# Rings of two to four buffers for the modulation pieces, and another spread of their sums over the stages

## The reference

```python
for layer in range(2):
    sh_m, sc_m, g_m, sh_f, sc_f, g_f = split(cond @ ada_w[layer] + ada_b[layer], 6)
    h = rms_norm(x, norm_w[layer, 0]) * (1.0 + sc_m) + sh_m
    y = even_mixer(h) if layer == 0 else odd_mixer(h)   # mLSTM + forgetting attention; GLA
    x = x + g_m * rms_norm(y, norm_w[layer, 1])
    h = rms_norm(x, norm_w[layer, 2]) * (1.0 + sc_f) + sh_f
    y = conv_ffn(h)          # 2048 -> 2 x 5632, causal conv of 3, a * gelu(g), 5632 -> 2048
    x = x + g_f * rms_norm(y, norm_w[layer, 3])
```

## Time and profile before

| | |
|---|---|
| Median of 3 runs | 2491.28 us (2486.13 to 2492.52) |
| Profiled execution, its own time | 2495.06 us |
| Its span | 2493.2 us |
| PE busy | 2389.3 us, 96% |
| DVE busy | 1994.6 us, 80% |
| ACT busy | 1007.4 us, 40% |
| DMA | 627 MB, 251 GB/s over the span |
| Granted clock of PE, mean | 0.990 |

### The profile page before, as it was taken

How to read it: one execution, slowest core, us unless ns; L and a number is a source line. 1 busy time by engine, 2 the same in 40 slices (tenths; PEclk the granted TensorE clock), 3 DMA queues, 4 the chain that set the end, 5 groups by cost and what they waited for, 6 DMA issues and landing times.

```text
span 2493.2 us, 36131 instructions
## 1 busy us (share of the span) xinstructions
PE 2389.3 (96%) x13994; PEld 2108.8 (85%) x13994; DVE 1994.6 (80%) x2531; ACT 1007.4 (40%) x1028; POOL 221.5 (9%) x111
## 2 busy tenths in 40 slices
PE   7999989799999999999989999998999999999998
PEld 6878877699988999799878888887888888888886
DVE  6779987789977998789777767777888778877875
ACT  2134444353333343333445544454444334433443
POOL 0000000024410443024200000000000000000000
PEclk9999999999999999999999999999999999999999
DMA  9999966857788777877858644466455865576553
GB/s 400 413 366 354 353 224 240 287 192 271 273 301 301 275 276 287 308 284 277 301 188 305 228 152 140 148 236 237 169 185 186 296 225 185 185 257 248 183 188 136
DMA packets 114466, 627.03 MB, mean 251 GB/s; under 512 B 12768, under 2 KB 12960, under 8 KB 63152
## 3 DMA queue, kind: packets, MB, share of 16 engines
q1 hardware_dynamic: 113648, 621.22, 68.5%
q10 hardware_dynamic: 704, 4.23, 0.4%
HBM read 623.27 MB, written 2.13 MB: 251 GB/s over the span
## 4 chain that ended last, share of the span: by engine, by line
PE 71%; DVE 15%; DMA 10%; ACT 3%; issue 1%; SPq 0%; DVEq 0%; ACTq 0%
PE bank L1760 17%; PE bank L1761 16%; PE bank L1756 7%; PE bank L1757 7%; PE bank L1784 7%; PE bank L1786 7%; PE bank L1785 7%; DMA piece<-ada_pieces 6%; DVE lo L934 5%; DVE piece L945 3%; DMA region<-ada_pieces 3%; ACT hi L507 2%; PE bank L1666 1%; DVE y L945 1%; PE bank L1540 1%
## 5 line engine op out<-in xcount | busy, mean ns | idle before, releaser
L507 ACT ACTIVATE hi<-raw 128x2048 fp32r<-128x2048 f32 x378 | 724.4, 1917 | 1116.4 <-PE bank L1761 678.8
L1761 PE MATMUL bank<-act,lo 128*128 128x256 f32 x3616 | 1020.1, 282 | 0.0
L934 DVE TENSOR_TENSOR lo<-raw,hi 128x2048 fp32r<-128x2048 f32 x378 | 864.9, 2288 | 144.2 <-ACT hi L507 143.3
L1761 PEld LDWEIGHTS bank<-act,lo 128*128 128x128 f32 x3616 | 690.0, 191 | 0.1
L1760 PE MATMUL bank<-act,hi 128*128 128x512 f32 x1920 | 678.0, 397 | 3.0 <-DVE lo L934 2.5
L1756 PE MATMUL bank<-act,hi 128*128 128x256 f32 x1696 | 485.0, 286 | 8.2 <-DVE lo L934 7.2
L1757 PE MATMUL bank<-act,hi 128*128 128x256 f32 x1696 | 481.7, 284 | 0.0
L945 DVE SCALAR_TENSOR_TENSOR piece<-piece,cond 128x1024 f32<-128x1024 f32 x290 | 398.0, 1375 | 83.2 <-DMA piece<-ada_pieces 83.0
L1760 PEld LDWEIGHTS bank<-act,hi 128*128 128x128 f32 x1920 | 360.3, 188 | 90.5 <-DVE lo L934 3.4
L1756 PEld LDWEIGHTS bank<-act,hi 128*128 128x128 f32 x1696 | 327.7, 193 | 11.5 <-issue 5.3
L1757 PEld LDWEIGHTS bank<-act,hi 128*128 128x128 f32 x1696 | 327.6, 193 | 0.1
(11 more groups left out here) (184 smaller groups left out, 1966.7 us busy)
## 6 DMA issues: line engine op xcount, KB each, us to landing
raw<-w_units SPq DMA_DIRECT2D x378, 1024.0 KB, 4.9
piece<-ada_pieces SPq DMA_DIRECT2D x290, 512.0 KB, 5.2
region<-ada_pieces SPq DMA_DIRECT2D x64, 512.0 KB, 13.9
raw<-head_units SPq DMA_DIRECT2D x16, 1024.0 KB, 16.0
y<-ada_pieces SPq DMA_DIRECT2D x30, 512.0 KB, 6.4
region<-gamma_scratch ACTq DMA_DIRECT2D x4, 1024.0 KB, 6.7
x<-x_in SPq DMA_DIRECT2D x1, 2048.0 KB, 9.2
x_out<-x SPq DMA_DIRECT2D x3, 512.0 KB, 2.8
```

The costliest lines, as they stand in the source:

```text
L507: sc.activation(hi[:, slot, :], raw[:, raw_slot, :], ACT.Copy).then_inc(s_hi, 1)
L934: ve.tensor_tensor(lo[:, slot, :], raw[:, raw_slot, :], hi[:, slot, :].bitcast(F32), ALU.subtract).then_inc(s_lo, 1)
L1761: i_ = pe.matmul(dst, w_lo, act[:, kt, 0:T], start=False, stop=at == DK - 1)
```

## The change

The pieces get ten slots in place of four, and each phase names a ring of them. Slots 0 and 1 are `piece`; 2, 3 and 7 lie in `y`; 4 and 5 in the place of the gamma row; 6 is `extra`; 8 and 9 are the places of the first GLA heads' queries and keys. The first `mixed` and the last first-layer `ff_down` have rings of three, the other two first-layer `ff_down` and the second `mixed` rings of four, the first `ff_up` and the decay phase of three, the GLA phases rings of two, other two than before. A slot is opened once by a load at a given place behind a wait for its last user, and after that each load follows the sum of the piece that lay in the slot before, even over phases.

The places of the sums move too. First-layer `ff_up` groups sum 24, 16 and 12 pieces where it was 32, 32 and 24. The first two `ff_down` sum 30 each where it was 24. The GLA phases sum 16 and 8 where it was none. All other counts stay. With three pieces per body the first `ff_up` is written out in full and not looped.

```diff
-    no, down = (0,) * 4, (1, 2, 2, 1) * 4
+    no, down = (0,) * 4, (1, 2, 2, 2, 2, 2, 2, 2) * 2
...
-              Phase("mixed", 0, 1, 16, (0, 0, 0, 1, 1, 2, 2, 2, 2, 2, 2, 2, 2, 2, 0, 0)),
-              Phase("ff_up", 0, 8, 4, (1,) * 4, 0), Phase("ff_down", 0, 1, 16, down, 0),
-              Phase("ff_up", 0, 8, 4, (1,) * 4, 1), Phase("ff_down", 0, 1, 16, down, 1),
-              Phase("ff_up", 0, 6, 4, (1,) * 4, 2),
-              Phase("ff_down", 0, 1, 12, (1, 2, 2, 1, 2, 2, 1, 2, 2, 1, 0, 0), 2),
+              Phase("mixed", 0, 1, 16, (0, 0, 0, 1, 1, 2, 2, 2, 2, 2, 2, 2, 2, 2, 0, 0), ring=(0, 1, ROWS)),
+              Phase("ff_up", 0, 8, 4, (1, 1, 1, 0), 0, ring=(0, 1, GAMMA)),
+              Phase("ff_down", 0, 1, 16, down, 0, ring=(0, 1, GAMMA, GAMMA + 1)),
+              Phase("ff_up", 0, 8, 4, (1, 0, 1, 0), 1),
+              Phase("ff_down", 0, 1, 16, down, 1, ring=(0, 1, GAMMA, GAMMA + 1)),
+              Phase("ff_up", 0, 6, 4, (1, 0, 1, 0), 2),
+              Phase("ff_down", 0, 1, 12, (1, 2, 2, 1, 2, 2, 1, 2, 2, 1, 0, 0), 2, ring=(0, 1, ROWS)),
...
-              Phase("columns", 1, 4, 4, (2, 1, 2, 1), dest=GQ, side="decay"),
-              Phase("values", 1, 2, 8, (0,) * 8, side="gla"),
-              Phase("columns", 1, 2, 8, (0,) * 8, dest=GR, side="gla", side0=2),
-              Phase("mixed", 1, 1, 16, (0, 0, 0, 0, 1, 1, 1, 2, 2, 2, 2, 2, 2, 1, 0, 0)),
+              Phase("columns", 1, 4, 4, (2, 1, 2, 1), dest=GQ, side="decay", ring=(0, 1, GAMMA)),
+              Phase("values", 1, 2, 8, (1,) * 8, side="gla", ring=STORED),
+              Phase("columns", 1, 2, 8, (0, 0, 1, 1, 1, 1, 0, 0), dest=GR, side="gla", side0=2, ring=HEADS),
+              Phase("mixed", 1, 1, 16, (0, 0, 0, 0, 1, 1, 1, 2, 2, 2, 2, 2, 2, 1, 0, 0), ring=HEADS + (0, 1)),
...
+        if ph.per_body % 2:
+            ph.head = ph.bodies
...
+OPENS = {(5, ROWS), (6, GAMMA), (7, GAMMA + 1), (11, ROWS), (13, GAMMA), (14, 3), (14, 7), (15, 8), (15, 9),
+         (16, 0), (16, 1)} | {(1, k) for k in EARLY}
+
+def piece_plan():
+    slots, uses, follows, opened = {}, {}, {}, {}
+    last, count = {}, [0] * ADA_SLOTS
+    for n, ph in enumerate(PHASES):
+        for a in range(ph.a0, ph.a_end):
+            slot = ph.ring[(a - ph.a0) % len(ph.ring)]
+            if (n, slot) in OPENS and last.get(slot, 0) < ph.a0:
+                opened[n, slot] = a
+            else:
+                follows[last[slot]] = a
+            slots[a], uses[a], last[slot] = slot, count[slot], a
+            count[slot] += 1
+    return slots, uses, follows, opened
...
-        pieces = [piece[:, 0, :], piece[:, 1, :], yf[:, 0:PIECE], yf[:, PIECE:2 * PIECE]]
+        pieces = [piece[:, 0, :], piece[:, 1, :], yf[:, 0:PIECE], yf[:, PIECE:2 * PIECE],
+                  gamma_row[:, 0:PIECE], gamma_row[:, PIECE:2 * PIECE], extra[:, :], yf[:, 2 * PIECE:3 * PIECE],
+                  region[:, GQ * T:GQ * T + PIECE], region[:, GK * T:GK * T + PIECE]]
...
+            def open_slots(number, ph, j):
+                if number == 5 and j == 0:
+                    sp.wait_ge(s["mlstm_scores_ready"], M_HEADS)
+                    load_piece(OPENED[5, ROWS], ROWS)
+                if number == 6 and j == 0:
+                    sp.wait_ge(s_yg, CHUNKS + 1)
+                    load_piece(OPENED[6, GAMMA], GAMMA)
+                if number == 7 and j == 0:
+                    load_piece(OPENED[7, GAMMA + 1], GAMMA + 1)
+                if number == 11 and j == 0:
+                    sp.wait_ge(s_evac, 2 + ph.t0)
+                    load_piece(OPENED[11, ROWS], ROWS)
+                if number == 13 and j == 0:
+                    sp.wait_ge(s_yg, 2 * (CHUNKS + 1))
+                    load_piece(OPENED[13, GAMMA], GAMMA)
+                    sp.wait_ge(s_act, 2 * 8)
+                    for slot in STORED:
+                        load_piece(OPENED[14, slot], slot)
+                if number == 15 and j == 1:
+                    sp.wait_ge(s["gla_level_product"], 2 * (LEVELS + 1))
+                    for slot in HEADS:
+                        load_piece(OPENED[15, slot], slot)
+                if number == 16 and j == 2:
+                    sp.wait_ge(s["gla_attended"], G_HEADS)
+                    for slot in PAIR:
+                        load_piece(OPENED[16, slot], slot)
...
                         for _ in range(ph.ada[j]):
                             a = ph.a0 + i * ph.per_body + k
...
+                            if ahead[k] > 0:
                                 sp.wait_ge(s_mac, a + 1)
-                                load_piece(a + ahead, slot)
+                                load_piece(a + ahead[k], ph.ring[k % len(ph.ring)])
                             k += 1
```

More of the change, by code:

```diff
@@ L45 @@
 SECTIONS = 6 * LAYERS
-ADA_SLOTS, EARLY_SLOTS = 2, 4
 HEAD_SLOTS = 8
@@ L55, with __init__ @@
 class Phase:
-    def __init__(self, kind, layer, bodies, units, ada, group=0, dest=0, side=None, side0=0):
+    def __init__(self, kind, layer, bodies, units, ada, group=0, dest=0, side=None, side0=0, ring=(0, 1)):
         self.kind, self.layer, self.bodies, self.units, self.ada = kind, layer, bodies, units, ada
@@ L147, with last_use, piece_ahead, even_loads @@
 PAUSE = next(ph for ph in PHASES if ph.side == "gla").a0
-EARLY_END = next(ph for ph in PHASES if ph.side == "mlstm").a0
-assert (EARLY_END - 2 * PIECES) % EARLY_SLOTS == 0
-def piece_slot(ph, k):
-    a = ph.a0 - 2 * PIECES + k
-    if ph.a0 < EARLY_END:
-        assert ph.bodies == 1 or ph.per_body % EARLY_SLOTS == 0
-        return a % EARLY_SLOTS, a // EARLY_SLOTS, ph.per_body // EARLY_SLOTS
-    early = EARLY_END - 2 * PIECES
-    return ((a - early) % ADA_SLOTS, early // EARLY_SLOTS + (a - early) // ADA_SLOTS, ph.per_body // ADA_SLOTS)
+FIRST = 2 * PIECES
+OPENS = {(5, ROWS), (6, GAMMA), (7, GAMMA + 1), (11, ROWS), (13, GAMMA), (14, 3), (14, 7), (15, 8), (15, 9),
[4 more added lines that the diff above has]
+    for n, ph in enumerate(PHASES):
+        assert ph.per_body % len(ph.ring) == 0 or ph.bodies == 1 or ph.side == "mlstm"
+        for a in range(ph.a0, ph.a_end):
[6 more added lines that the diff above has]
+            count[slot] += 1
+    assert set(opened) == OPENS
+    return slots, uses, follows, opened
+SLOT, USE, FOLLOWS, OPENED = piece_plan()
+def last_use(slot, before):
+    return max(a for a in SLOT if SLOT[a] == slot and a < before)
+def piece_ahead(ph, i):
+    return [FOLLOWS.get(a, a) - a for a in range(ph.a0 + i * ph.per_body, ph.a0 + (i + 1) * ph.per_body)]
+def even_loads(ph):
+    return all(piece_ahead(ph, i) == piece_ahead(ph, ph.head) for i in range(ph.head, ph.bodies - ph.peel))
 V_ADAB = 0
@@ L454, in _, with body @@
             sp.wait_ge(s_hact, DK)
[L455 to L456 removed]
+            for slot in EARLY[2:4]:
+                load_piece(FIRST + slot, slot)
             sp.wait_ge(s_lo, RAW_SLOTS + 1)
             load_unit(RAW_SLOTS, 0)
[L460 to L461 removed]
+            def open_slots(number, ph, j):
[24 more added lines that the diff above has]
+                        load_piece(OPENED[16, slot], slot)
+            for number, ph in enumerate(PHASES):
+                def body(i, ph=ph, number=number):
+                    ahead = piece_ahead(ph, ph.now)
                     k = 0
@@ L489, in _ @@
                     sp.wait_ge(s["mlstm_stored"], 2 + M_HEADS)
+                    sp.wait_ge(s_mac, last_use(ROWS, PAUSE) + 1)
                     sp.dma_start(g_w2, w2_dram).then_inc(s["loaded_a_w2"], 16)
-                straight = ph.per_body > 0 and ph.a_end in (PAUSE, SECTIONS * PIECES)
-                kept, ph.peel = ph.peel, max(ph.peel, int(straight))
+                kept = ph.head, ph.peel
+                ph.head = max(ph.head, int(any(at[0] == number for at in OPENS)))
+                while not even_loads(ph):
+                    ph.peel += 1
                 repeat(sp, ph, body)
-                ph.peel = kept
+                ph.head, ph.peel = kept
             for k, (tb, at, size) in enumerate(X_PIECES):
```

44 lines of the change are left out of this document (17 added, 27 removed).

## The result

The changed kernel takes 2461.32 us in the median of four runs (2454.18 to 2463.43), the kernel before 2488.9 us (four runs, 2486.13 to 2492.52). The ratio is 0.9883 with an interval of 0.9858 to 0.9909, so the change takes away 1.2%, well beyond the 0.3% that can be told from nothing. The profiled execution took 2454.18 us with a span of 2452.4.

The account below looks back on a forecast made before the run. PE, busy for 96% of the span, bounds the kernel; waits for pieces cost it at most 43.3 us. Terms sum to -33.5 us, giving 2458 us against 2491.28, range 2448 to 2472.

Parts of the forecast that it names:

- The ceiling at PE: Seven places where waits for pieces reach PE, against undisturbed stages of the same work: gain at most 43.3 us.
- Rings of four in `ff_down`: First two `ff_down`: slots return in 10.9 us, added sums are covered, 0.5 us kept in each: -5.7 and -4.3 us.
- The seams: From `ff_down` to second and third `ff_up`: first piece may be late, but only once; 1.2 of 2.1 us taken back.
- Rings of three: First `mixed` and third `ff_down`: landing just met in the median, 3.0 and 2.5 us kept: -11.6 and -6.0 us.
- Ring of four in the second `mixed`: Second `mixed`: four pieces wait in slots before the first sum, 1.1 of 7.1 us kept: -6.0 us.
- GLA, +1.3: Twenty-four sums in GLA: most fit DVE's idle time, two crowded places and the columns cost +1.3 us.
- The rivals: Four other outcomes: (a) 2472 us, 0.11; (b) 2464, 0.10; (c) 2485, 0.06; (d) 2499, 0.03.
- (a): DMAs are full at 352 GB/s, both long `ff_down` stay about as they are: 2472 us, chance 0.11.
- (b): Three slots too few at 8.1 us landings, 0.76 us over a unit, gain falls by 6.5: 2464 us, chance 0.10.
- (c): GLA exposes every sum, 24 x 1.2 = 29 us in place of 1.3: 2485 us, chance 0.06.
- (d): Slower: exposed GLA sums also bring half-clock windows, 13.6 us more than the 29: 2499 us, chance 0.03.
- The signs: Profile after: piece waits from 83 to under 20 us, long `ff_down` 87 each, landings near 8, GLA at most 2 longer.

Follow-up runs that it names:

- the rings alone: Changed kernel with its new rings, but sums and the slot counts of `ff_up` and GLA as before: 2458.63 us, 0.9878 of the kernel before.
- the other counts: Changed kernel with third `ff_down` counts (2, 2, 2, 1, 1, 1, 2, 2, 2, 1, 0, 0) and sums moved in `ff_up` and GLA: 2460.19 us.
- more load: Changed kernel with two further unread loads of 256 KB per unit in the first two `ff_down`: 2490.04 us in one run.
- the best kernel: New rings with old sum places, plus a fourth slot in the first `mixed` and new third `ff_down` counts: 2455.78 us, 0.9863 of the kernel before.

## Why the prediction was right

*The ceiling at PE, 43.3 us.* Right as a method, a little large in size. The same reckoning on the second profile of before gives 12.3 for the first `mixed` (66.0 - 53.7), 2.6 for the first `ff_down` (88.9 - 86.3) and 10.4 for the third (75.2 - 64.8), where the prediction had 14.6, 6.2 and 8.5. With 4.1, 6.6 and 2.1 for the second `ff_down`, the second `mixed` and the two seams, all from the table, that is 38. The prediction knew that its execution was 3.8 us above the median, yet took its terms whole and subtracted them from the median. The ceiling also contained the clock, and that part came back: before, three windows of 3.4 us in the two `mixed` had half the clock, the one of the earlier trace rows and these two,

```profile
485.70:489.10 3.40, 3.14 (x7) 2.51 (x8) 2.41 (x2) 0.03 (x1) 0.00 (x0) 0.50 0.77 255
1711.10:1714.50 3.40, 3.40 (x10) 2.66 (x9) 3.12 (x5) 0.00 (x0) 0.00 (x0) 0.51 0.84 276
```

and after, both stages have the full clock:

```profile
388.50:478.90 90.40, 88.42 (x384) 70.99 (x382) 77.11 (x78) 37.87 (x33) 0.00 (x0) 1.00 0.80 307
1600.00:1689.80 89.80, 89.33 (x393) 73.22 (x392) 71.41 (x70) 39.08 (x35) 0.00 (x0) 1.00 0.77 282
```

PE was busy for 9.9 us in the three windows, so by my estimate up to 5.0 us of the gain are the clock, which went to half behind these stalls and does not without them.

*Rings of four in `ff_down`, -5.7 and -4.3.* Right: -6.1 and -4.7 against the first profile of before, -2.5 and -4.1 against the second. The 0.5 us that I kept in each was not needed. The six added sums per stage cost nothing, as PE stays at 86.4 us with them and without them.

*The seams, -1.2.* Half right. The third `ff_up` gives 1.5. At the second one, -0.6, +1.8 or -0.5 us were found against the first profile of before, and +0.7, +3.1 or +0.8 against the second, since one piece is still late there. The time line of DVE in the changed kernel:

```profile
777.22 1.23 DVE L1004 SCALAR_TENSOR_TENSOR piece<-piece,cond 128x1024 f32<-128x1024 f32 x1 [2.81 <-DMA piece<-ada_pieces]
```

With one sum in every unit, or none in the first, this wait isn't there. In the second profile of the changed kernel it was 3.7 us, and a window of 3.4 us at a granted clock of 0.51 followed it (787.6 to 791.0), which makes that stage the longest, 187.9. I had named the piece behind the seam, but not that the counts decide it.

*Rings of three, -11.6 and -6.0.* Right in the sum (-19.4 between the first profiles, -18.4 from the second profile of before to the mean of the last two after), and right that a ring of three does not give all of it: the changed kernel keeps 0.3 to 2.7 us of the first `mixed` over the 93.5 of a ring of four, and other kernels with that ring of three up to 4.7; 3.0 were predicted. The third `ff_down` keeps 3.1 in the first profile where 2.5 were predicted, but by another way than I had thought. Its one long wait, with the units around it even:

```profile
1213.70 1.29 DVE L1522 TENSOR_TENSOR y<-y,bank 128x512 f32<-128x512 f32 x2 [0.21 <-PE bank L1846]
...
1217.52 1.23 DVE L1004 SCALAR_TENSOR_TENSOR piece<-piece,cond 128x1024 f32<-128x1024 f32 x1 [2.53 <-DMA piece<-ada_pieces]
```

The pieces of that unit were issued from 1209.03 us on. One microsecond earlier, at 1208.12, ACT's queue issued the load of the gamma row, 1 MB. Issue to landing, of that load and then of the two pieces behind it:

```profile
DMA to landing us min/median/max: 8.3/8.3/8.3
...
DMA to landing us min/median/max: 8.5/8.5/8.6
```

Three slots tolerate the 6.6 us of an ordinary landing, not these 8.5. In four more profiles with this ring and these counts (the changed kernel twice more, the rings alone, and the kernel with three slots in the long `ff_down`), the two pieces behind the gamma row landed after 7.3 to 9.1 us, and the wait that followed was 1.4 to 3.0 us. With the other counts in the third `ff_down`, this unit takes 5.44 us and not 7.7. That the gamma row is the cause is read from the order of the loads; it was not moved by itself.

*Ring of four in the second `mixed`, -6.0.* -7.0 and -6.6; nothing is left to be had there.

*GLA, +1.3.* 0.9 us were found, all of it in one unit of the second head, the crowded one that was named, which goes from 6.6 to 7.7 us. Moving that one sum brings it back to 6.6 and the values to 110.0. The columns stay at 117.0.

*The rivals.* (a), full DMAs, did not come true: PE is busy for all 87 us of both `ff_down`, and under more load the DMAs reach 396 GB/s. Its sum had slips that nearly cancel: at 92.4 us each the two `ff_down` would have lost 1.2 us and not gained 1, and the second `mixed` would have gained 4 and not 3. (b), three slots, is real in kind but too dear. It kept 7 us in the first `mixed` and 5 in the third `ff_down`, where the changed kernel's profiles keep 0.3 to 2.7 us over a ring of four and 1.9 to 3.1 over the 64.8 us that PE's pace gives; in the long `ff_down` three slots cost 2.0 to 3.6 us in sixteen units and not 0.76 a unit. (c) and (d) ask for 24 exposed sums; doubling the sums costs 10.2 us and a single one 0.9.

*The signs.* Waits for pieces fell to 11.0 us (under 20 was predicted), both long `ff_down` take 87 us, with landings of 7.2 us and not near 8, and GLA is 0.9 us longer in all (at most 2 was predicted).

*The sum.* -33.5 us was set against 2491.28. The end of the last unit moved by -40.9 between the first profiles, and by -26.9 from the second profile of before (2473.8) to the mean of the last two of the changed kernel (2447.6, 2446.3). The first pair has a share of luck: 2.5 of its 40.9 us lie in the second layer's second `ff_up`, which the change does not touch. The stages that the prediction named moved by -38.4 in that pair and by -30.3 in the other, on either side of -33.5. The medians moved by 27.6, 31.3 and 27.4 in three comparisons. The predicted 2458 us lies 1.9 to 3.8 below the three medians of the changed kernel, inside its range, and the reason is the first point above.

## What to carry to other kernels

Read a stall that comes from a DMA at the engine that sets the end, stage against undisturbed stage of the same work, and do it on two profiles: such stalls vary by several microseconds a stage from one execution to the next. The depth of a ring follows from the time between a slot's release and its next use, against the slowest landing under the load that the change itself creates (here 7.2 us in the median and 8.5 behind a 1 MB load, where a median of 5.6 was seen before), and one slot more than just enough also takes spread out of the times. A stall can cost more than its length, since time at half clock may follow it. Once the rings are deep enough, where the filler work stands within stages in which PE sets the pace brings nothing; it only loses where the filler's engine has no idle time, or right behind a seam.

## What had not been expected of the hardware

The columns units of the second layer run at one of two paces. In its second `ff_up`, where nothing waits for pieces in either kernel, the changed kernel took 178.1 us from first to last start in one execution and 180.7 in the next. The first profile, whole and from 2029.7 us on, and then the same kernel again:

```profile
L1821 PE MATMUL bank<-act,lo x512: 277/280/284, 1974.7 to 2152.8; 128*128 128x256 f32 x171
...
L1821 PE MATMUL bank<-act,lo x356: 280/280/280, 2029.7 to 2152.8; 128*128 128x256 f32 x178
```

```profile
L1821 PE MATMUL bank<-act,lo x512: 277/281/284, 1978.2 to 2158.9; 128*128 128x256 f32 x171
```

A unit takes 5.65 us at first in both, and in the first profile 5.55 from the tenth on, at a granted clock of 1.00. Both profiles of the kernel before have 180.9 in the table and stay at 5.65 us. It changes the other way too: in the second layer's first `ff_up` the kernel before has 5.55 us nearly throughout (180.7 us from first to last start), and the second profile of the best kernel goes over to 5.65 after the seventh unit (183.8). In the first layer's second and third `ff_up` every unit from the fourth on takes 5.76 us, in all kernels. I found no wait or load that goes with these changes. They are worth up to 3 us a stage and so add to the spread of the times; their cause stays open.

The other one is the 396 GB/s of the kernel with more load, beside the 413 of the earlier trace rows: scaling the 306 GB/s of the first `ff_down` before, at a share of 0.87, up to 352 for a full share was wrong. The same stage moved 359 at 0.95 after the change and 396 at 1.00 under more load, so a share below one with stalls in between told little of the rate at a full share.
